# First layer of a fused two-block transformer kernel: GpSimd, VectorE and ScalarE work issued in another order

## What is computed

```python
for layer in range(2):
    proj = rms_norm(h, g1) @ w_in      # u_ssm | u_g | v_g | q | k | v
    y_ssm  = s5_mixer(u_ssm, ...)      # a_bar = exp(lam*dt); b_bar = ((a_bar-1)/lam) * b; scan; gelu; glu
    y_sgu  = spatial_gating(u_g, v_g)
    y_diff = diff_attention(q, k, v)   # norm of q and k heads, rotary, softmax(s1) - lam * softmax(s2)
    h = h + concat(y_ssm, y_sgu, y_diff) @ w_out[layer]
    h = h + conv_gated_mlp(rms_norm(h, g2))
x = second_block(h, mem, ...)          # one layer, not touched
```

## Time and profile before

| | |
|---|---|
| time, median of 3 runs | 1007.24 us (1007.22 to 1008.64) |
| time of the profiled execution | 1008.24 us |
| its span, first to last instruction | 1006.4 us |
| TensorE busy | 977.6 us of the span |
| VectorE, ScalarE, GpSimd busy | 704.0, 547.8, 249.7 us |
| granted TensorE clock, mean | 0.996 of full speed |

### The profile page before, as it was taken

One profiled execution on the slowest core, in us unless ns is written; L12 is line 12 of the kernel. 1 busy time (PEld: TensorE's weight loads), 2 busy tenths in 40 slices (PEclk: granted clock), 3 DMA queues, 4 the chain that ended last, 5 costly groups with the idle time before them and its releaser, 6 DMA issues.

```text
span 1006.4 us, 15915 instructions
## 1 busy us (share of the span) xinstructions
PE 977.6 (97%) x6214; PEld 855.9 (85%) x6214; DVE 704.0 (70%) x1072; ACT 547.8 (54%) x898; POOL 249.7 (25%) x196
## 2 busy tenths in 40 slices
PE   6989999999999999999999999999999999999997
PEld 4868789999977887889999988999877789888786
DVE  6998557799854688656677846557667755666785
ACT  7645546666644655645576545545354454555723
POOL 4890102688300021102425300003122300000030
PEclk9989999999999999999999999999999999999999
DMA  8622355555565553256555665665545445855452
GB/s 297 207 84 85 89 184 179 181 171 185 187 186 152 169 165 126 67 149 218 185 189 183 178 190 161 189 209 172 182 137 158 146 134 162 217 153 155 146 185 84
DMA packets 48474, 165.97 MB, mean 165 GB/s; under 512 B 6544, under 2 KB 7056, under 8 KB 48400
## 3 DMA queue, kind: packets, MB, share of 16 engines
q1 hardware_dynamic: 48400, 164.95, 52.6%
HBM read 162.83 MB, written 1.05 MB: 163 GB/s over the span
## 4 chain that ended last, share of the span: by engine, by line
PE 84%; DVE 10%; ACT 2%; issue 1%; POOL 1%; DMA 1%; DVEq 0%; POOLq 0%; SPq 0%; ACTq 0%
PE PJ L578 13%; PE PJ L580 13%; PE PJ L579 13%; PE PJ L571 10%; PE PJ L573 10%; PE PJ L572 10%; DVE wlo L1665 3%; PE PJ L534 2%; PE PJ L536 2%; PE PJ L535 2%; PE T L1008 1%; PE PJ L695 1%; PE T L999 1%; PE T L773 1%; DVE ropeq L1776 1%
## 5 line engine op out<-in xcount | busy, mean ns | idle before, releaser
L1665 DVE TENSOR_TENSOR wlo<-raw,whi 128x1024 fp32r<-128x1024 f32 x294 | 377.9, 1316 | 96.0 <-ACT whi L1067 93.8
L1067 ACT ACTIVATE whi<-raw 128x1024 fp32r<-128x1024 f32 x294 | 303.4, 1061 | 71.4 <-DMA raw<-weights_in 65.4
L571 PE MATMUL PJ<-xth,whi 128*128 128x256 f32 x864 | 245.3, 284 | 2.1 <-DVE wlo L1665 1.3
L572 PE MATMUL PJ<-xtl,whi 128*128 128x256 f32 x864 | 244.5, 283 | 0.0
L573 PE MATMUL PJ<-xth,wlo 128*128 128x256 f32 x864 | 244.5, 283 | 0.0
L578 PE MATMUL PJ<-whi,xth 128*128 128x512 f32 (+1 forms) x432 | 175.6, 406 | 5.5 <-DVE wlo L1665 3.4
L571 PEld LDWEIGHTS PJ<-xth,whi 128*128 128x128 f32 x864 | 165.8, 192 | 3.4 <-issue 3.2
L580 PE MATMUL PJ<-whi,xtl 128*128 128x512 f32 (+1 forms) x432 | 168.2, 389 | 0.0
L579 PE MATMUL PJ<-wlo,xth 128*128 128x512 f32 (+1 forms) x432 | 168.0, 389 | 0.0
L572 PEld LDWEIGHTS PJ<-xtl,whi 128*128 128x128 f32 x864 | 165.8, 192 | 0.2
L573 PEld LDWEIGHTS PJ<-xth,wlo 128*128 128x128 f32 x864 | 165.8, 192 | 0.0
(11 more groups left out here) (398 smaller groups left out, 1384.0 us busy)
## 6 DMA issues: line engine op xcount, KB each, us to landing
raw<-weights_in SPq DMA_DIRECT2D x294, 512.0 KB, 3.5
rt<-bmerge_in SPq DMA_DIRECT2D x6, 256.0 KB, 4.1
xres<-x_in SPq DMA_DIRECT2D x2, 512.0 KB, 5.3
xn<-mem_in SPq DMA_DIRECT2D x2, 512.0 KB, 5.4
y_out<-xn SPq DMA_DIRECT2D x4, 256.0 KB, 2.4
rowv<-rows_in SPq DMA_DIRECT2D x1, 576.0 KB, 10.2
ptmp<-bexp_in SPq DMA_DIRECT2D x2, 256.0 KB, 5.8
cex<-cexp_in SPq DMA_DIRECT2D x2, 256.0 KB, 8.1
```

Of the source, the lines that this page charges most:

```text
L571: pe.matmul(o, a, xh[:, k, :], start=(first and f % 2 == 0), stop=False, skip_group_check=True)
L572: pe.matmul(o, a, xl[:, k, :], start=False, stop=False, skip_group_check=True)
L1067: act.activation(whi[:, p % HIGHS, :], raw[:, p % LOADS, :], ACT.Copy).then_inc(hi_ready, 1)
L1665: dve.tensor_tensor(wlo[:, p % LOADS, :], raw[:, p % LOADS, :], whi[:, p % HIGHS, :].bitcast(F32), ALU.subtract).then_inc(lo_ready, 1)
```

## The change

In words: the attention mask constants land in `kT` (free until k is evacuated) instead of in `cst`, so that GpSimd can write `ident4` and `skip` into `cst` without waiting for ScalarE's copy of the masks; this makes one DMA two. GpSimd makes those constants between the roots of the two tiles, the amplitude powers before the second tile's root, and then waits for the rotary tables before `input_powers`. Behind `input_powers` it runs the decay table, `fold_coefficient`, the first `output_powers`, both head roots, and the second `output_powers`. VectorE makes the phase factors before the first tile is scaled, the rotary tables behind lo 3 (before `norm_lo` of tile 1), and the coefficients right behind lo 6, where the rotary tables were. TensorE runs one gmlp pair ahead of `input_products` and the transposes of b one pair sooner; ScalarE makes the phase tables before one of its `whi`. At the end of the first layer's mixing VectorE makes lo 24 and lo 25 behind the last two `mix_low` instead of ahead of them.

```diff
--- before.py
+++ after.py
...
         st_ = sbt(mix, "st_", [P, 3, 8, 4])
+        mdiff = kT[:, 0:2, :].rearrange("p f n -> p (f n)")[:, 0:384]
         sv = qh[:, :, :, :].rearrange("p a b (s c) -> p (a b s) c", c=NC).rearrange("p (k s) c -> p k s c", k=4)
...
-            n_par, n_id = COL["conv"][0], CST["ident"][1]
+            n_par, n_id, n_mask = COL["conv"][0], CST["ident"][1], CST["mdiff"][0]
             small(colv[:, 0:n_par], cols[:, 0:n_par], "par_landed")
...
                 if p == 4:
-                    small(cst[:, n_id:NCST], consts[:, n_id:NCST], "cst_landed")
+                    small(cst[:, n_id:n_mask], consts[:, n_id:n_mask], "cst_landed")
+                    small(mdiff[:], consts[:, n_mask:NCST], "cst_landed")
                     small(rowv[:], rows.to_broadcast([P, NROW]), "cst_landed")
...
                     tile_pairs(f"q{l}", 0, j, range(4), xth, xtl, ready=32 * l, upto=j + 1)
-                    if l == 0 and j == 1:
+                    if l == 0 and j == 0:
                         b_transposes(0, B[:, 0, :])
...
                     shuffle_in()
+                    project("gmlp0", pairs=[0])
                     input_products()
-                    project("gmlp0", pairs=[0, 1])
+                    project("gmlp0", pairs=[1])
                     head_transposes(1, (S0, S1))
...
                 squares(0, xres, 1, half)
+            hi_upto(3)
+            b_evac(0, PJ[buf("k0")][:, 0, :])
             hi_upto(4)
-            b_evac(0, PJ[buf("k0")][:, 0, :])
             norm_hi(0, 1)
             hi_upto(6)
-            act.wait_ge(sem("cst_landed"), 32)
+            act.wait_ge(sem("cst_landed"), 48)
             act.copy(identb[:, :], ident).then_inc(sem("maskb_ready"), 1)
...
                 act.copy(maskb[:, t, :].rearrange("p (h n) -> p h n", h=k),
-                         wide(cs("mdiff")[:, 0:128] if t == 0 else cs("mdiff")[:, 128:384], k)).then_inc(sem("maskb_ready"), 1)
+                         wide(mdiff[:, 0:128] if t == 0 else mdiff[:, 128:384], k)).then_inc(sem("maskb_ready"), 1)
...
                 act.copy(uc[:, :, :], A[:, 1, :]).then_inc(sem("uc_ready"), 1)
-                hi_upto(s0 + 17)
+                hi_upto(s0 + 16)
                 if l == 0:
                     phase_tables(act, 0)
+                hi_upto(s0 + 17)
                 act.wait_ge(sem("qk_tr"), 2 * l + 2)
...
                     if l == 0:
-                        act.wait_ge(sem("par_ready"), 5)
+                        act.wait_ge(sem("par_ready"), 6)
                     for t in range(TT):
...
-            def norm_rstd(n):
+            def norm_rstd(n, tiles=range(TT)):
...
                     link(pool.tensor_scalar(ssm1[:, n, :], ssq[:, n, 0:4:2], D * EPS, None, ALU.add))
-                for t in range(TT):
+                for t in tiles:
                     pool.wait_ge(sem("ssq_ready"), 4 * n + (2 * t + 2 if n in AT_ONCE else 3 + t))
...
-            def folded(l):
+            def skip_rows(l):
...
                     link(pool.tensor_scalar(skip[:, f * P:(f + 1) * P], ident, col("dskip", 2 * l + f, 1), None, ALU.mult))
-                if l == 0:
-                    pool.wait_ge(sem("par_ready"), 4)
-                fold_coefficient(pool, link, l, ptmp)
...
             link(pool.memset(mT[:], 0.0))
-            norm_rstd(0)
+            norm_rstd(0, (0,))
+            pool.wait_ge(sem("ident_landed"), 16)
+            link(pool.tensor_tensor(skip[:, 0:64], ident[:, 0:64], ident[:, 64:128], ALU.add))
+            link(pool.tensor_tensor(skip[:, 0:32], skip[:, 0:32], skip[:, 32:64], ALU.add))
+            link(pool.tensor_copy(ident4.rearrange("p (t h) -> p t h", t=STEP), wide(skip[:, 0:32], STEP)))
+            pool.wait_ge(sem("par_landed"), 16)
+            skip_rows(0)
             pool.wait_ge(sem("par_ready"), 3)
             amplitude_powers()
+            norm_rstd(0, (1,))
             pool.wait_ge(sem("bex_ready"), 1)
+            pool.wait_ge(sem("par_ready"), 4)
             input_powers(pool, link, 0, 0, x_tile(0), ptmp)
             input_powers(pool, link, 0, 1, x_tile(1), ptmp)
-            head_powers(0, 0)
             link(pool.tensor_tensor(sp_[:, 20, :], sp_[:, 3, :], sp_[:, 3, :], ALU.mult))
...
             pool.sem_inc(sem("decay_ready"), 1)
-            pool.wait_ge(sem("maskb_ready"), 3)
-            link(pool.tensor_tensor(skip[:, 0:64], ident[:, 0:64], ident[:, 64:128], ALU.add))
-            link(pool.tensor_tensor(skip[:, 0:32], skip[:, 0:32], skip[:, 32:64], ALU.add))
-            link(pool.tensor_copy(ident4.rearrange("p (t h) -> p t h", t=STEP), wide(skip[:, 0:32], STEP)))
-            folded(0)
+            pool.wait_ge(sem("par_ready"), 5)
+            fold_coefficient(pool, link, 0, ptmp)
+            output_powers(pool, link, 0, 0, ptmp)
+            head_powers(0, 0)
             head_powers(0, 1)
-            output_powers(pool, link, 0, 0, ptmp)
             output_powers(pool, link, 0, 1, ptmp)
...
                         if j == 5:
-                            folded(l + 1)
+                            skip_rows(l + 1)
+                            fold_coefficient(pool, link, l + 1, ptmp)
                         if j in (6, 7):
...
             dve.sem_inc(sem("par_ready"), 1)
+            link(dve.tensor_scalar(v[19], v[5], 2.0 / math.pi, None, ALU.mult))
+            link(dve.tensor_scalar(v[18], v[19], MAGIC, None, ALU.add))
+            link(dve.tensor_scalar(v[18], v[18], -MAGIC, None, ALU.add))
+            link(dve.tensor_tensor(v[19], v[19], v[18], ALU.subtract))
+            link(dve.memset(chunks[:, :], 1.0))
+            link(dve.tensor_tensor_scan(chunks[:, :], chunks[:, :], chunks[:, :], -1.0, ALU.mult, ALU.add))
             norm_scale(0, xres, 0)
             lo_upto(1)
-            norm_lo(0, 0)
-            lo_upto(2)
             dve.wait_ge(sem("par_a"), 4)
...
             v[15] = apw[:, 1, 1, :]
+            norm_lo(0, 0)
             lo_upto(3)
...
             lo_upto(4)
-            link(dve.tensor_scalar(v[19], v[5], 2.0 / math.pi, None, ALU.mult))
-            link(dve.tensor_scalar(v[18], v[19], MAGIC, None, ALU.add))
-            link(dve.tensor_scalar(v[18], v[18], -MAGIC, None, ALU.add))
-            link(dve.tensor_tensor(v[19], v[19], v[18], ALU.subtract))
-            link(dve.memset(chunks[:, :], 1.0))
-            link(dve.tensor_tensor_scan(chunks[:, :], chunks[:, :], chunks[:, :], -1.0, ALU.mult, ALU.add))
+            dve.wait_ge(sem("cst_landed"), 48)
+            cosv = cs("cos").rearrange("p (t d) -> p t d", t=TT)
+            sinv = cs("sin").rearrange("p (t d) -> p t d", t=TT)
+            def rotation_rows(l):
+                for i, (g, tb_) in enumerate((("qg", cosv), ("qg", sinv), ("kg", cosv), ("kg", sinv))):
+                    link(dve.tensor_tensor(ropeq[:, i, :, :], tb_, wide(row(g, 64 * l, 64), TT), ALU.mult))
+            rotation_rows(0)
+            dve.sem_inc(sem("par_ready"), 1)
             norm_lo(0, 1)
             lo_upto(7)
-            dve.wait_ge(sem("cst_landed"), 32)
-            cosv = cs("cos").rearrange("p (t d) -> p t d", t=TT)
-            sinv = cs("sin").rearrange("p (t d) -> p t d", t=TT)
...
                 s0 = slot(f"q{l}")
-                for i, (g, tb_) in enumerate((("qg", cosv), ("qg", sinv), ("kg", cosv), ("kg", sinv))):
-                    link(dve.tensor_tensor(ropeq[:, i, :, :], tb_, wide(row(g, 64 * l, 64), TT), ALU.mult))
-                lo_upto(s0 + (9 if l else 7))
+                if l:
+                    rotation_rows(l)
+                    lo_upto(s0 + 9)
+                else:
+                    coefficients()
...
                 rotary(0, A, "q_terms", "q_rot", s0 + (10 if l else 9))
-                if l == 0:
-                    lo_upto(s0 + 10)
-                    coefficients()
                 lo_upto(s0 + 11)
...
                 diff_norm(1)
-                lo_upto(s0 + 26)
+                lo_upto(s0 + (26 if l else 24))
                 mix_low(4, S1[:, :], 3)
```

## The result

| | before | after |
|---|---|---|
| median, 15 runs each | 1007.78 us | 1009.97 us |
| range | 1007.05 to 1009.29 | 1009.14 to 1011.29 |
| span of the profiled execution | 1006.4 us | 1008.1 us |
| TensorE busy | 977.6 us | 979.0 us |

The ratio is 1.0021, 95% interval 1.0014 to 1.0027: slower by 2.2 us, with +1.7 forecast. The forecast of 1008.9 us stood on the three-run median of 1007.24; on the fifteen-run median of 1007.78 the same +1.7 is 1009.5. The two spans differ by 1.7 us.

The account below looks back on a forecast made before the run. TensorE, busy 97% of the span, bounds the kernel; only its waits, where VectorE is late, and low clock can give much. Terms +0.1 +3.1 −1.5 sum to +1.7 us: 1008.9 us, range 1002.5 to 1012.0.

Parts of the forecast that it names:

- Turns: VectorE operations with both inputs in SBUF wait out whole GpSimd operations, and vice versa; a rotary operation loses 1.84 us.
- Start, +0.1: At the first scaling (7.98 us), GpSimd's five early constants may slip ahead: 0 to 0.3 us, taken as 0.1.
- Coefficients and lo 7, wait 2.1: Coefficients behind lo 6 end at 36.0, lo 7 is ready at 38.3; TensorE waits 2.1 us at pair 7.
- Fold to 41.0, lo 8 another 1.0: GpSimd's fold ends at about 41.0, lo 8 is ready at 42.1; TensorE waits 1.0 us more behind pair 7.
- Lo 9, wait 5.4: First output powers collide with rotary and lo 9, ready at 50.45; TensorE waits 5.4 us at pair 9 from 45.0.
- Low clock 2.8: The 2.8 us of TensorE's low clock, before behind the lo 14 wait, come behind the pair 9 wait instead.
- Scaled k, no wait, at 67.1: VectorE finishes scaling k at 67, TensorE reaches its transposes at about 67.1, so no wait there.
- The slower rival: Second powers win the turn ahead of lo 12 and k's scaling; everything 2.3 us later, +4.0, 1011.2 us; chance 0.2.
- Scores end at 75.3, lo 15 waits 1.3, pair 15 ends at 82.2: TensorE ends scores at 75.3, waits 1.3 us for lo 15, ends pair 15 at 82.2 instead of 79.1: 3.1 late.
- Low parts, −1.5: End of first layer's mixing: moving two lo operations behind the low parts removes a 1.5 us TensorE wait.
- The faster rival: Behind the fold, turns cost VectorE much less (half rate or late powers); 1001.7 us, half of it 1004.5; chance 0.25.

Follow-up runs that it names:

- the halves: Changed kernel with each of the three operations of the first output powers cut into two of 128x512: 1004.90 us, ratio 0.9973.
- the fastest version: Changed kernel with coefficients, roots and gmlp pair back in old places, lo 15 ahead of lambda operations, only first output powers in halves: 1002.23 us, ratio 0.9957.
- the one execution above: Profiled, slowest execution of the changed kernel with coefficients, roots, gmlp pair back, all output powers halved, lo 15 ahead of lambda operations; median 1003.10 us.

## Why the prediction came out, step by step

- *Turns.* Right, and now shown apart from its rival by the halves. It was too narrow in one word: I wrote of operations with both inputs in SBUF, but L343, one SBUF input, takes 2.08 us beside a power and 0.43 alone, and the scaling of tile 1, which reads one too, took 2.29 us in the kernel with the tables back and 0.88 otherwise. The page of the Trainium skill cited ahead ("GPSIMD Engine Reference", Key points) also names VectorE's two-port modes; no run here tells whether L343 is in one.
- *Start, +0.1.* The first scaling begins at 7.79 instead of 7.98, but that is the execution's: its x landed 0.26 us sooner, and in the other traces of the same code the scaling begins at 7.76 to 8.23. It follows the root by 0.11 us instead of 0.03, so the term is 0.08, as good as said.
- *Coefficients and lo 7, wait 2.1.* 2.29. The coefficients ended at 35.7 (36.0 said).
- *Fold to 41.0, lo 8 another 1.0.* The fold ended at 40.86 and lo 8 at about 41.9 (42.1 said). The 1.0 us wait did not come, and this step failed in part: I let the clock fall only behind waits as long as the 3.2 us of the earlier trace rows, and it fell behind 2.29. Pair 7 ran at 1.2 GHz and took 4.4 us instead of 2.8, to 42.76. So in place of 1.0 us of waiting 1.6 us went into slow matmuls; that the sum still holds is in part luck.
- *Lo 9, wait 5.4.* 4.36; lo 9 ready at 50.1 (50.45 said). TensorE came there at 45.8 instead of 45.0, which is the difference but for 0.3.
- *Low clock 2.8.* Pair 9 took 5.3 us instead of 2.9, so 2.4, and the transposes behind it 1.27 instead of 1.03.
- *Scaled k, no wait, at 67.1.* At 66.86, scaled at 66.5. The slower rival did not happen, but by 0.3 us only: the second powers took turns with L343, L344 and lo 12 (3.38 us), and not with the scaling itself (1.21). I made that rival hang on GpSimd's root ending before VectorE is through rotary for k, and my own times, 57.1 and 57.4, met its condition. Measured they are 57.2 and 56.9, the other way round, so the first phase operation still slipped through (0.69). That the scaled k was in time is in part luck.
- *Scores end at 75.3, lo 15 waits 1.3, pair 15 ends at 82.2.* 74.8, 1.38, 82.0. The place before, which I put at 79.1, was 78.92, so the 3.1 stands.
- *Low parts, −1.5.* The wait is gone.

The sum +3.1 −1.5 stands in the traces as +3.1 at pair 15 and −1.5 at the low parts. It stands although two terms inside the 3.1 were off, the wait ahead of lo 8 and that at pair 9 (4.36, not 5.4), since slow matmuls took their place. The faster rival is out: both rotary operations lost 1.8 us, not 0.6. What I had not priced is that the change without its early coefficients and order of the roots gains some 2.1 us beyond the low parts. In the changed kernel nothing is left of it: the coefficients stand where the tables stood and take the same three turns, and let the powers go ahead of lo 9.

## To carry to other kernels

Where two engines take turns, as VectorE and GpSimd do here, price a moved operation by whom it meets, not by its own length: list both engines' instructions side by side and count all the meetings (there were six in the experiment with the roots first). A helper engine's long elementwise instructions belong beside work that the other engine does from PSUM, and cutting them into halves shortens each turn but prolongs the time in which turns are taken, so small operations ahead of an urgent one must go behind it. An engine that is freed early may be worse than one that is late: GpSimd's powers behind the early coefficients, and `input_powers` at 16.60 without the wait for the tables, both cost time. And when a piece is moved back to price it, look at what waits went with it.

## What was not expected of the hardware

TensorE's clock fell to 1.2 GHz behind waits much shorter than the 3.2 us seen in the kernel before: behind 2.29 us in the changed kernel (matmuls 0.43 apart instead of 0.23 for some 3 us) behind 2.22 us with the coefficients back, behind 1.96 us in the fastest version and 1.89 us with the first powers in halves. It stayed full behind the 1.38 us ahead of pair 15, and behind 1.78 us in the kernel before. In the one execution above it fell behind 1.1 us and stayed low for some 10 us. What decides it stays open.
